# Mixer scores: levels under 32 as 32x32 blocks summed to one tile before the product with v

## The reference, cut to what matters

```
def step(S, inp):
    qi, ki, vi, gi = inp
    bcum = jnp.cumsum(gi, axis=2)
    b_last = bcum[:, :, -1:, :]
    o_inter = jnp.einsum('bhtd,bhde->bhte', qi * jnp.exp(bcum), S)
    diff = bcum[:, :, :, None, :] - bcum[:, :, None, :, :]
    decay = jnp.where(causal, jnp.exp(jnp.minimum(diff, 0.0)), 0.0)
    att = jnp.einsum('bhtd,bhtsd,bhsd->bhts', qi, decay, ki)
    o = o_inter + jnp.einsum('bhts,bhse->bhte', att, vi)
    S = jnp.exp(b_last[:, :, 0, :])[..., None] * S + jnp.einsum(
        'bhsd,bhse->bhde', ki * jnp.exp(b_last - bcum), vi)
    return S, o
```

## Time and profile before

| | |
|---|---|
| three runs | 4444.16, 4440.14, 4441.54 us |
| median | 4441.54 us |
| span of the profiled execution | 4444.5 us |
| TensorE busy | 4093.7 us, 92% |
| VectorE busy | 3686.2 us, 83% |
| ScalarE busy | 1732.4 us, 39% |
| the HGRN2 mixer | from about 95 to 619 us |
| the GLA mixer | from about 2326 to 2747 us |

### The profile page before, as it was taken

One profiled execution on the slowest core, in us unless ns is written; L12 is line 12 of the kernel. 1 busy time (PEld: TensorE's weight loads), 2 busy tenths in 40 slices (PEclk: granted clock), 3 DMA queues, 4 the chain that ended last, 5 costly groups with the idle time before them and its releaser, 6 DMA issues. The chain is left out here.

```text
span 4444.5 us, 73738 instructions
## 1 busy us (share of the span) xinstructions
PE 4093.7 (92%) x24855; PEld 3709.2 (83%) x24855; DVE 3686.2 (83%) x6798; ACT 1732.4 (39%) x2584; POOL 1899.2 (43%) x1320
## 2 busy tenths in 40 slices
PE   6899988968999999999988997895899999999997
PEld 3899977847899999999977887884799999999997
DVE  6688864998788888999987885498788888999997
ACT  6455533427333333333334443222633333333333
POOL 2100014737545445556552122222644544566664
PEclk9899978989999999999998997897999999999999
DMA  7111123519999999999972112110999999999995
GB/s 288 52 50 55 58 72 119 178 34 225 360 363 363 361 363 355 364 365 360 362 266 59 39 51 74 52 54 9 253 366 361 364 360 363 357 361 363 363 360 222
DMA packets 620190, 1049.51 MB, mean 236 GB/s; under 512 B 229763, under 2 KB 405318, under 8 KB 619590
## 3 DMA queue, kind: packets, MB, share of 16 engines
q1 hardware_dynamic: 471520, 508.69, 34.0%
q0 software_dynamic: 147456, 536.94, 32.3%
q10 hardware_dynamic: 1126, 2.79, 0.2%
HBM read 982.75 MB, written 65.54 MB: 236 GB/s over the span
## 5 line engine op out<-in xcount | busy, mean ns | idle before, releaser
L2083 POOL DMA_INDIRECT rows_ex<-in_peer_v,ctx_index x512 | 703.6, 1374 | 479.7 <-DVE row_acc_ex L2162 364.1
L2083 POOL DMA_INDIRECT rows_ex<-in_peer_u,ctx_index x512 | 586.8, 1146 | 635.4 <-DVE dots_ex L2165 502.4
L2248 PE MATMUL pu_ex<-h_hi,uT_hi_ex 128*128 128x384 f32 x2048 | 715.8, 350 | 1.9 <-ACT coef_ex L2112 1.0
L2162 DVE SCALAR_TENSOR_TENSOR row_acc_ex<-rows_ex,factor_ex,row_acc_ex 128x1024 f32<-128x1024 f32 x512 | 657.7, 1284 | 56.3 <-issue 17.6
L2248 PE MATMUL pu_ex<-h_lo,uT_hi_ex 128*128 128x384 f32 x2048 | 692.8, 338 | 0.0
L2248 PE MATMUL pu_ex<-h_hi,uT_lo_ex 128*128 128x384 f32 x2048 | 692.8, 338 | 0.0
L2256 PE MATMUL py_ex<-v_hi_ex,c_hi_ex 128*128 128x512 f32 x1536 | 622.5, 405 | 0.0
L2165 DVE CUSTOM_DVE_ANT_0 rows_ex<-rows_ex,h_row_ex 128x1024 f32<-128x1024 f32 x512 | 604.2, 1216 | 0.0
L2256 PE MATMUL py_ex<-v_lo_ex,c_hi_ex 128*128 128x512 f32 x1536 | 601.0, 391 | 0.0
L2256 PE MATMUL py_ex<-v_hi_ex,c_lo_ex 128*128 128x512 f32 x1536 | 600.6, 391 | 0.0
L2101 ACT ACTIVATE uT_hi_ex<-pT_ex 128x512 fp32r<-128x512 f32 x512 | 304.0, 594 | 509.4 <-PE pT_ex L2241 486.2
(11 more groups left out here) (446 smaller groups left out, 8422.9 us busy)
## 6 DMA issues: line engine op xcount, KB each, us to landing
u_raw_ex<-in_peer_u SPq DMA_DIRECT2D x256, 512.0 KB
v_raw_ex<-in_peer_v SPq DMA_DIRECT2D x256, 512.0 KB
gates<-stage_ro SPq DMA_DIRECT2D x12, 4096.0 KB, 16.0
g_raw_ex<-gates SPq DMA_DIRECT2D x256, 192.0 KB
ada<-in_ada_w SPq DMA_DIRECT2D x12, 2048.0 KB, 11.8
ada_re<-in_ada_w SPq DMA_DIRECT2D x16, 1536.0 KB, 6.8
w_raw_hgrn<-in_hgrn_w_in SPq DMA_DIRECT2D x40, 512.0 KB
w_raw_re<-in_peer_w_q SPq DMA_DIRECT2D x32, 512.0 KB, 5.7
```

Of the source, the lines that this page charges most:

```text
L2083: pool.indirect_dma_start(out=rows[m % RING][:, :], out_offset=None, in_=a["peer_u" if m < TG * NC else "peer_v"].rearrange("l n d -> (l n ...
L2162: nc.vector.scalar_tensor_tensor(row_acc[g][:, :], rows[j][:, :], factor[:, j:j + 1], row_acc[g][:, :], ALU.mult, ALU.add).then_inc(row_fr ...
L2248: last_ = nc.tensor.matmul(pu[:, 0:TD], w[:, k, :], x[:, k, 0:TD], start=(k == 0 and w is uT_hi[b] and x is h_hi), stop=(k == DC - 1 and w ...
```

## The change

The levels under 32 (3 to 6) and the diagonal only have entries in the 32x32 blocks along the diagonal of a tile. They are now computed as four 32x32 blocks each, which go to four column groups of TensorE; `pA` keeps 128 columns for levels 0 to 2 and has 5 x 32 columns for the rest (`fine_tiles`). VectorE multiplies the 160 columns by `fine_mask` into `fm` and sums the five to `near`, 128 x 32 (`gather_near`). ScalarE spreads `near` to all four column blocks of `am`, now 128 x 128 (`spread_near`). VectorE overwrites `am` where `coarse_mask` is set with the first 128 columns of `pA` (`copy_predicated`). Where neither belongs (other 32-blocks of small exclusive or) the coarse mask takes the coarse value. TensorE then has one product with v in place of six.

```diff
@@ mixer: tiles
-        am = [sb(f"am{i}", [P, NM, P]) for i in range(2)]
+        am = [sb(f"am{i}", [P, P]) for i in range(2)]
+        fm = sb("fm", [P, NF, FINE])
+        near = [sb(f"near{i}", [P, FINE]) for i in range(2)]
@@ mixer: views
+        def score_tile(t):
+            return pA[t % 2][:, :, :].rearrange("p a b -> p (a b)")
+        def fine_tiles(t):
+            return score_tile(t)[:, P:P + NF * FINE].rearrange("p (l j) -> p l j", j=FINE)
+        def by_block(x):
+            return x.rearrange("p (b j) -> p b j", j=FINE)
@@ mixer: ScalarE, head
+                def spread_near(t):
+                    act.wait_ge(near_done, h * NT + (t + 1))
+                    act.wait_ge(o_done, h * NT + (1 + (t - 1 if t >= 2 else 0)))
+                    act.activation(by_block(am[t % 2][:, :]),
+                                   near[t % 2][:, :].unsqueeze(1).to_broadcast([P, P // FINE, FINE]), ACT.Copy) \
+                        .then_inc(near_out, 1)
+                spread_near(0)
+                spread_near(1)
                 if not final:
                     decays(h + 1, h + 1)
                 for t in range(NT):
                     act.wait_ge(o_done, h * NT + (1 + t + 1))
                     act.activation(oT[:, bass.ds(h * NV, NV), t * P:(t + 1) * P],
                                    pO[:, 0:NV, :], ACT.Copy).then_inc(o_out, 1)
+                    if t + 2 < NT:
+                        spread_near(t + 2)
                     if t == 2 and not final:
                         log_f(h + 1)
@@ mixer: VectorE, head
+                def gather_near(t):
+                    dve.wait_ge(att, h * NT + (t + 1))
+                    nc.vector.tensor_mul(fm[:, :, :], fine_tiles(t), c["fine_mask"][:, :, :])
+                    dve.drain()
+                    if t >= 2:
+                        dve.wait_ge(near_out, h * NT + (t - 1))
+                    nc.vector.tensor_reduce(near[t % 2][:, :], fm[:, :, :].rearrange("p l j -> p j l"), AX.X, ALU.add) \
+                        .then_inc(near_done, 1)
+                    dve.drain()
+                gather_near(0)
+                gather_near(1)
                 for t in range(NT):
-                    dve.wait_ge(att, h * NT + (t + 1))
-                    dve.wait_ge(o_done, h * NT + (1 + (t - 1 if t >= 2 else 0)))
-                    nc.vector.tensor_mul(am[t % 2][:, :, :], pA[t % 2][:, 0:NM, :], c["level_mask"][:, :, :]) \
-                        .then_inc(masked, 1)
+                    if t >= 1 and t + 1 < NT:
+                        gather_near(t + 1)
+                    dve.wait_ge(near_out, h * NT + (t + 1))
+                    alone(dve, dve_passed)
+                    nc.vector.copy_predicated(am[t % 2][:, :], c["coarse_mask"][:, :].bitcast(U16),
+                                              score_tile(t)[:, 0:P]).then_inc(masked, 1)
@@ mixer: TensorE, level_scores, own_scores, output
-                        tok = slice(t * P, (t + 1) * P)
-                        nc.tensor.matmul(pA[t % 2][:, l - 2, :], ex[:, 1, l, tok], ex[:, 0, l, tok], start=True, stop=True)
+                        for r in range(0, P, FINE):
+                            tok = slice(t * P + r, t * P + r + FINE)
+                            nc.tensor.matmul(fine_tiles(t)[r:r + FINE, l - 3, :], ex[:, 1, l, tok], ex[:, 0, l, tok],
+                                             start=True, stop=True)
...
-                        terms = [(tt[:, 10 + t * NV + vv, :], am[t % 2][:, l, :]) for l in range(NM)]
+                        terms = [(tt[:, 10 + t * NV + vv, :], am[t % 2][:, :])]
```

More of the change, by code:

```diff
@@ L10 @@
 U32 = mybir.dt.uint32
+U16 = mybir.dt.uint16
 I32 = mybir.dt.int32
@@ L28 @@
 NL = len(LEVELS)
-NM = NL - 1
+FINE = 32
+NF = NL - 2
 DEPTH = 2
@@ L1174, in level_scores @@
                         for r, col, n in blocks:
-                            nc.tensor.matmul(pA[t % 2][r:r + n, 0, col:col + n], ex[:, 1, l, t * P + r:t * P + r + n],
+                            nc.tensor.matmul(score_tile(t)[r:r + n, col:col + n], ex[:, 1, l, t * P + r:t * P + r + n],
                                              ex[:, 0, l, t * P + col:t * P + col + n], start=True, stop=True)
                     else:
-                        tok = slice(t * P, (t + 1) * P)
-                        nc.tensor.matmul(pA[t % 2][:, l - 2, :], ex[:, 1, l, tok], ex[:, 0, l, tok], start=True, stop=True)
+                        for r in range(0, P, FINE):
+                            tok = slice(t * P + r, t * P + r + FINE)
+                            nc.tensor.matmul(fine_tiles(t)[r:r + FINE, l - 3, :], ex[:, 1, l, tok], ex[:, 0, l, tok],
+                                             start=True, stop=True)
                 def own_scores(t):
-                    tok = slice(t * P, (t + 1) * P)
-                    nc.tensor.matmul(pA[t % 2][:, NM - 1, :], kd[:, tok], q[:, tok], start=True, stop=True) \
-                        .then_inc(att, 1)
+                    for r in range(0, P, FINE):
+                        tok = slice(t * P + r, t * P + r + FINE)
+                        last = nc.tensor.matmul(fine_tiles(t)[r:r + FINE, NF - 1, :], kd[:, tok], q[:, tok],
+                                                start=True, stop=True)
+                    last.then_inc(att, 1)
                 def scores(t):
```

18 lines of the change are left out of this document (11 added, 7 removed).

## The result

| | before | after |
|---|---|---|
| time, median (range), same chip | 4442.5 us (4440.1 to 4444.2) | 4499.8 us (4499.1 to 4502.3) |
| ratio after / before, 95% interval | | 1.013 (1.0118 to 1.0142) |
| span of the profiled execution | 4444.5 us | 4497.1 us |
| mean granted clock of TensorE | 0.951 | 0.927 |

What follows compares the result with a forecast made beforehand. The bound was taken to be the tail's chain of waits to the next head's scan, not TensorE's total work. 21 + 6 + 2.5 - 2.5 - 6 = +21 us on 4441.5, rounded to 4462 us; range 4437 to 4484 us.

Steps and rivals of the forecast that it cites:

- Setup: Before the first scan: building smaller masks while inputs load costs nothing, between -1 and +1 us.
- The HGRN2 tails: From last level factor to next head's scan: +3.0 us per head in seven tails, +21 us.
- the clock: TensorE's granted clock may fall in idle HGRN2 tails; half of 1.86 us taken, 0.9 us per head, +6 us.
- The chain of waits: HGRN2 tail on ScalarE: spreads delay sigmoids and logarithm, output 0's copy waits behind sigmoids; scan +3.0 us per head.
- Rival 1: TensorE's clock falls in every tail and stays low: +35 us, 4477 us; chance 0.17, over +30.
- VectorE's pieces: Per tile on VectorE: product 0.33, sum 0.33, predicated copy 0.29 us; with drains 1.26 us for 0.88 before.
- rivals 4 and 5: VectorE's new work per tile cheap, 0.5 us: 4427 us, chance 0.1; or expensive, 2.2 us: 4484 us, chance 0.08.
- GLA: Three GLA heads with a next head: VectorE sets the time, +0.8 us each, +2.5 us.
- Last heads: Last HGRN2 and last GLA head, where TensorE's work was the path: -2.5 and -6 us.
- The mixers' sum: All HGRN2 and GLA heads with the clock's cost: 21 + 6 + 2.5 - 2.5 - 6 = +21 us.
- Rival 3: TensorE bounds the kernel, and VectorE's front part shrinks when inputs come earlier: -57 us, 4385 us; chance 0.05.
- The 131 us of work: TensorE work removed by shorter scores and fewer v products in all heads: 8 x 9 + 4 x 14.7 us.

## Why the prediction was wrong, and where it was right

**The step that failed** is "Setup builds smaller masks while inputs load; I take nothing, between -1 and +1 us". It priced the instructions that build the masks (the first scan is 1.0 us later, the edge of that range; over all runs it lies between 153.4 and 155.5 us) and not the masks' size. 960 bytes less move each later tile, and the gate stores of the route stage start at an address that is no multiple of 256. The runs with and without padding show it from both sides: 31 to 33 us back in the changed kernel, 36 us lost in the kernel before. No rival of the prediction named it. Nothing in the trace of before announces it but the size of the packets, 256 bytes, and a DMA queue at 290 GB/s that was little short of setting the pace of its stage (a store landed in 16.0 us, and the next was issued 17.4 us behind it).

**The HGRN2 tails.** Forecast were +21 and +6 for the clock, measured +30.5. Step by step in the tail shown, from the last factor: first gather forecast +0.6, measured +0.53; table load +2.7 and +2.83; output 0 +2.9 and +2.90; L1009 +6.8 and +6.93; output 1 +7.6 and +7.88, behind an idle stretch of 3.11 us where 2.9 were forecast; L1014 +10.8 and +11.65. Of those 0.85 us, 0.28 were there at output 1, and most of the rest is scores 3 at half clock, 1.49 us for 1.1. The scan is at +20.49 for +19.6. So this tail is 3.8 us longer, and forecast were 3.0 and 0.9 for the clock. The chain of waits was right: the spreads ahead of the sigmoids, the spread ahead of the logarithm, the copy of output 0 behind both. Over all seven, tails grew by 29.4 us, 4.2 each: the five in which the clock fell earlier are 0.6 us and more longer than this one. The front parts, which the forecast had held free, grew by 1.1 us in all.

**The clock.** Half of 1.86 us per head was taken, 6 us. Rival 1, that the clock falls in every tail and stays low, was what happened in HGRN2, and it put 13 us on the seven tails. TensorE kept busy gave back 6.5 us in the tails, near the 6 that were taken, though its products also stand in the way of others. It gave 3.6 us in the seven periods as a whole, and 12 in the kernel. That the right size came with the wrong case (half of the price in doubt, and not a fall in every tail) is in part luck. And the clock's price depends on what else is late: 0.5 us per head while ScalarE's sigmoids are late too, 2.3 us (428.2 to 412.0 us in seven periods) once they are not; the forecast had one price for both. The rule cited from the Trainium skill, "TensorE: Matmul & The Clock Gate", Part 1 (throttled by default, released by activity), agrees with the granted clock of 0.50 at the end of all seven tails.

**VectorE's pieces.** The product and the predicated copy came out within 0.01 us. The sum took 0.425 us and not 0.33: it reads its 160 columns with a stride of 32, and the earlier trace rows had a sum of another shape, which may be why; no run varied it. That is 0.1 us per gather; rivals 4 and 5 (cheap and expensive pieces) are out.

**GLA** +2.5 forecast, +3.0 measured, with v's wait gone. **Last heads** -2.5 and -6 forecast, -1.0 and -8.8 measured: HGRN2 ran at half clock (period 4.52 us; the forecast had 5.1), GLA partly not (3.96 us; the forecast had 3.95 at full clock). The mixers' sum, +24.7 for +21, so hides errors of either sign: +3.5 in the HGRN2 heads that have a next one, +1.5 and -2.8 in the two last heads, +0.5 in GLA and +1.0 ahead of the first scan.

**Rival 3**, that TensorE is the bound, is refuted: it lost 79 us of busy time and the mixers grew. But the half of the change that shortens scores did help, by 16 us, through the waits for scores that the earlier trace rows show. (The 131 us of work have a slip of 1 us in them: by its own terms GLA's part is 4 x 14.5 us.) The sentence of the Trainium skill on the PSUM copy as the next bottleneck ("TensorEngine Tiling (Array Packing)", PSUM Bottleneck) fits the changed kernel, where VectorE's part per tile grew; with VectorE's part left alone the gain of the scores came through.

**Still open.** With the spread on GpSimd and TensorE busy, the sum to one tile still costs some 7 us over the scores-only kernel (ratios 0.9977 against 0.9961). By the profiles it is 12.8 us in the seven HGRN2 periods, 1.8 each, and the last GLA head gives 6.8 back. The trace names one piece: in each of the seven tails the first L1009 took 1.71 us, where it takes 0.61 in the other kernels (0.85 with GpSimd alone), and GpSimd was at its weight split then. VectorE waited at most 0.20 us at a time from there to the scan, so these 1.1 us count. That the split is what slowed it, no run tests, and the rest may be VectorE's longer chain of product, sum and predicated copy, which no run took apart. Open is also why the store's rate falls to the same 218 GB/s for every start that is no multiple of 256.

## What to carry to other kernels

A change of a constant's size is a change of the address of all that is allotted after it; look at every DMA with packets of a few hundred bytes whose queue is near full, and keep its SBUF side at a multiple of 256 bytes, by padding if need be. When an engine's work is cut, ask whether anyone waited for it, and what the idle stretch does to its clock. Then look at the next head too: a shorter tail at half clock came back as a longer front part. Two edits that gave 8 and 12 us alone gave 32 together, so an edit that "does nothing" may be one half of one that does. Split a change that pairs a cheap gain with a costly one, and time the halves.
